# State space groups of a two-block layer: decay arguments by TensorE instead of reloaded rows, centre tap on ScalarE

## The reference, cut to what matters

```python
def depthwise_conv(u, w, b):                     # 5 taps, centre tap is k = 2
    y = lax.conv_general_dilated(u, w.astype(u.dtype), window_strides=(1,), padding=[(pad, pad)], ...)
    return y + b.astype(u.dtype)

def segsum_exp(a):
    cs = jnp.cumsum(a, axis=-1)
    diff = cs[..., :, None] - cs[..., None, :]
    ...
    return jnp.exp(jnp.where(mask, diff, -jnp.inf))      # mask: lower triangle

def ssd_scan(x, dt, a, b, c):
    ...
    xdt = x * dt[..., None]
    decay = segsum_exp(a_dt)
    cb = jnp.einsum('bclgn,bcsgn->bcgls', c, b)
    y_diag = jnp.einsum('bcgls,bcgrls,bcsgrp->bclgrp', cb, decay, xdt)
    decay_states = jnp.exp(a_cs[..., -1:] - a_cs)
    states = jnp.einsum('bclgn,bcgrl,bclgrp->bcgrpn', b, decay_states, xdt)
    ...                                                   # scan over the 4 chunks
    y_off = jnp.einsum('bclgn,bcgrpn,bcgrl->bclgrp', c, prev, jnp.exp(a_cs))
    return (y_diag + y_off).reshape(Bsz, S, G, R, P)
```

## Time and profile before

| | us |
|---|---|
| median of 3 runs (lowest, highest) | 2027.85 (2026.93, 2028.11) |
| the profiled execution itself | 2022.01 |
| its span in the trace | 2020.2 |
| PE busy | 1840.2 (91%) |
| DVE busy | 971.5 (48%) |
| ACT busy | 795.3 (39%) |
| POOL busy | 842.3 (42%) |
| mean granted clock of PE | 0.964 of full |

### The profile page before, as it was taken

The page is one execution under the profiler, slowest core; times in us unless marked ns, Lnnn a source line. Parts: engine busy times, 40 slices in busy tenths (PEclk is TensorE's granted clock), DMA queues, the critical chain, the costliest instruction groups (busy, mean ns, idle before and its releaser), DMA issues.

```text
span 2020.2 us, 27117 instructions
## 1 busy us (share of the span) xinstructions
PE 1840.2 (91%) x8948; PEld 1517.4 (75%) x8948; DVE 971.5 (48%) x1312; ACT 795.3 (39%) x1627; POOL 842.3 (42%) x598
## 2 busy tenths in 40 slices
PE   5598898899789999998899999999989999889988
PEld 4477777677578787877788888877878888777766
DVE  4389888999930555423532022232082211545654
ACT  4233333333232465532343233334433332456542
POOL 4244443344734312243454444444484444442212
PEclk9899999999889999999999999999999999999989
DMA  4742223323113311132233323323222223221101
GB/s 153 137 145 60 87 89 98 104 83 104 42 53 94 110 60 61 52 136 75 82 94 94 101 98 94 96 92 136 93 83 84 83 85 103 73 87 33 62 31 52
DMA packets 55011, 176.76 MB, mean 87 GB/s; under 512 B 5291, under 2 KB 7723, under 8 KB 54668
## 3 DMA queue, kind: packets, MB, share of 16 engines
q1 hardware_dynamic: 38592, 140.53, 21.8%
q10 hardware_dynamic: 16332, 35.11, 6.4%
HBM read 169.19 MB, written 6.42 MB: 87 GB/s over the span
## 4 chain that ended last, share of the span: by engine, by line
PE 61%; DVE 19%; issue 12%; POOL 3%; ACT 3%; ACTq 1%; DVEq 1%; DMA 0%; POOLq 0%
PE main L294 47%; DVE dmat L1747 4%; PE aux L754 3%; PE main L322 2%; POOL w_lo L257 2%; DVE u_acc L1716 2%; PE aux L619 1%; PE aux L741 1%; DVE y_all L1787 1%; PE aux L728 1%; PE aux L364 1%; DVE dmat L1752 1%; DVE x_res L536 1%; PE aux L729 1%; PE aux L1628 1%
## 5 line engine op out<-in xcount | busy, mean ns | idle before, releaser
L257 POOL TENSOR_TENSOR w_lo<-raw,w_hi 128x512 fp32r<-128x512 f32 x504 | 708.0, 1411 | 1044.3 <-ACT w_hi L253 1026.7
L253 ACT ACTIVATE w_hi<-raw 128x512 fp32r<-128x512 f32 x486 | 302.5, 630 | 713.0 <-PE main L294 708.2
L294 PE MATMUL main<-w_hi,a_hi 128*128 128x512 f32 x752 | 320.2, 426 | 2.3 <-ACT vv L1350 1.4
L294 PE MATMUL main<-w_hi,a_lo 128*128 128x512 f32 x752 | 300.9, 400 | 0.0
L294 PE MATMUL main<-w_lo,a_hi 128*128 128x512 f32 x752 | 300.7, 400 | 0.0
L294 PE MATMUL main<-a_hi,w_hi 128*128 128x512 f32 x640 | 259.7, 406 | 2.2 <-ACT u_raw L1159 2.2
L294 PE MATMUL main<-a_hi,w_lo 128*128 128x512 f32 x640 | 252.5, 394 | 0.0
L294 PE MATMUL main<-a_lo,w_hi 128*128 128x512 f32 x640 | 252.4, 394 | 0.0
L294 PEld LDWEIGHTS main<-w_hi,a_lo 128*128 128x128 f32 x752 | 145.7, 194 | 32.5
L294 PEld LDWEIGHTS main<-w_hi,a_hi 128*128 128x128 f32 x752 | 146.5, 195 | 30.4 <-issue 1.9
L294 PEld LDWEIGHTS main<-w_lo,a_hi 128*128 128x128 f32 x752 | 146.6, 195 | 24.5
(11 more groups left out here) (278 smaller groups left out, 2997.8 us busy)
## 6 DMA issues: line engine op xcount, KB each, us to landing
raw<-w_stream_in SPq DMA_DIRECT2D x264, 512.0 KB, 3.5
dmat<-cs_rows ACTq DMA_DIRECT2D x32, 512.0 KB, 9.1
x_res<-x_in ACTq DMA_DIRECT2D x8, 512.0 KB, 4.9
rel_rows<-rel_row ACTq DMA_DIRECT2D x1, 4096.0 KB, 44.8
bias<-rel_rows ACTq DMA_DIRECT2D x2, 1536.0 KB, 7.8
out<-x_res SPq DMA_DIRECT2D x4, 512.0 KB, 2.6
bgate<-b_gate_in ACTq DMA_DIRECT2D x4, 256.0 KB, 5.7
ln_g<-ln_g_in ACTq DMA_DIRECT2D x1, 1024.0 KB, 6.7
```

The lines of the kernel that those rows point to most:

```text
L253: eng.activation(w_hi[:, k, :], raw[:, k, :], ACT.Copy).then_inc(hi_done, 1)
L257: eng.tensor_tensor(w_lo[:, k, :], raw[:, k, :], w_hi[:, k, :].bitcast(F32), ALU.subtract).then_inc(lo_done, 1)
L294: mm = eng.matmul(mb[m][:, :], lhs, rhs, start=(first and k == 0 and n == 0), stop=(last and k == KT - 1 and n == 2))
```

## The change

The cumulated sums no longer go through HBM.
- The transposed sums (64 rows: direction, group, head) are kept on chip in `cs_hl`: a rounded high part in partitions 0 to 63 (ACT copy) and the remainder in 64 to 127 (DVE). `pick` is a 0/1 table whose column (direction, group, head) has ones at the row of that high part and of its remainder; `pick_rows` copies a group's 8 columns into `picked`.
- `pe_arg(g, r)` is new on PE: one picked column, broadcast to 128 columns as the stationary operand, times `cs_hl` spreads head r's row over all partitions, direction 0 into aux2 and direction 1 into aux3. It takes both banks, so it waits for both `aux_free`, and whoever uses the banks next waits for `arg_done`.
- `take_arg` on ACT copies aux2 into e_buf with the (negated) per-token sum as bias, one instruction for each of the 4 chunks. `arg_min` on DVE adds the other direction's per-token sum to aux3 and takes the minimum with e_buf, again one instruction per chunk. Then `decay_exp` and `weigh` go on as before; dmat only holds weigh's result.
- `load_decay` and its waits are gone. ACT's wait for the bias rows of the later attention (`rel_stored`) now stands behind the last group.
- `centre` puts the centre tap and the bias of the convolution on ACT (Identity with scale and bias); DVE's `conv` keeps the 16 other taps.
- Each engine's list is written anew: arguments 0 and 1 of a group are made during the group before (slots 8 and 10), 2 and 3 in the group itself (slots 1 and 4).

```diff
+        cs_hl = at("cs_hl", B0 + 60 * KB, [P, TOK], FR)
+        pick = at("pick", B0 + 63 * KB, [P, 64])
+        picked = at("picked", B0 + 63 * KB + 256, [P, 2, 2, R], FR)
...
-        def load_decay(eng, g, r):
-            ...
-            eng.dma_start(dmat[r][:, :, :], src).then_inc(decay_landed[r], 16)
...
+        def pe_arg(eng, g, r, half):
+
+            if r == 0:
+                eng.wait_ge(pick_set, g + 1)
+
+            if not (isinstance(g, int) and g == 0 and r == 0):
+                for b in range(2):
+                    eng.wait_ge(aux_free[b], g * 5 + r)
+            for dr in range(2):
+                one_row = picked[:, half, dr, r:r + 1].broadcast_to((P, P))
+                x = eng.matmul(ab[2 + dr][:, :], one_row, cs_hl[:, :], start=True, stop=True)
+            x.then_inc(arg_full, 1)
+
+        def pe_turn(eng, g, part, half):
             bank = part % 2
+            eng.wait_ge(arg_done, g * 4 + (part // 2 + 1))
...
+        def pe_states(eng, g, i, half):
             if i == 0:
                 eng.wait_ge(xw_done, g * 2 + 2)
+            eng.wait_ge(arg_done, g * 4 + (3 + i // 2))
...
+            def centre(g, taken, pair):
+
+                two = TILES[2 * pair:2 * pair + 2]
+                act.wait_ge(bank_free, taken + (max(two) + 1))
+                for m in two:
+                    act.activation(u_acc[:, m, :], u_raw[:, m, :], ACT.Identity, bias=par[:, bass.ds(g * 4 + (PC["conv_b"] + m), 1)],
+                                   scale=par[:, bass.ds(g * 20 + (PC["conv_w"] + m * 5 + 2), 1)]).then_inc(centred, 1)
+
+            def take_arg(g, r):
+
+                act.wait_ge(arg_full, g * 4 + (r + 1))
+                if not (isinstance(g, int) and g == 0 and r < 2):
+                    act.wait_ge(t_done, g * 4 + (r - 1))
+                for c in range(NT):
+                    cs = slice(c * P, c * P + P)
+                    x = act.activation(e_buf[r % 2][:, cs], ab[2][:, cs], ACT.Identity, bias=cs_sb[:, c, bass.ds(g * R + r, 1)])
+                x.then_inc(arg_in, 1)
...
             take_x(0)
+            centre(0, 0, 0)
+            centre(0, 0, 1)
             hi(2, range(0, 3))
+            take_arg(0, 0)
             for n in range(4):
                 silu(0, n)
             hi(2, range(3, 6))
-            act.wait_ge(cs_stored, 16)
-            for r in range(R):
-                load_decay(act, 0, r)
             take_turned(0, 0)
+            take_arg(0, 1)
             hi(2, range(6, 7))
             take_turned(0, 2)
             take_turned(0, 3)
             take_x(1)
             hi(2, [7])
+            decay_exp(0, 0)
+            decay_exp(0, 1)
...
                     silu(g + 1, 2)
                     silu(g + 1, 3)
+                    take_arg(g + 1, 0)
                     slots(9, 10)
                     take_turned(g + 1, 0)
                     slots(10, 11)
+                    take_arg(g + 1, 1)
                     if half == 1:
                         take_x(gp * 3 + (P_Z + 2))
+                    decay_exp(g + 1, 0)
+                    decay_exp(g + 1, 1)
                     slots(11, 12)
                     take_turned(g + 1, 2)
                     take_turned(g + 1, 3)
...
+            def arg_min(g, r):
+
+                dve.wait_ge(arg_in, g * 4 + (r + 1))
+                for c in range(NT):
+                    e = e_buf[r % 2][:, c * P:c * P + P]
+                    x = dve.scalar_tensor_tensor(e, ab[3][:, c * P:c * P + P], cs_sb[:, c, bass.ds(g * R + (NH + r), 1)], e,
+                                                 ALU.add, ALU.min)
+                x.then_inc(arg_done, 1)
...
-                decay(0)
-                decay(1)
                 weigh(0)
+                if not last:
+                    pick_rows(g + 1, 1 - half)
+                arg_min(g, 2)
                 weigh(1)
-                decay(2)
-                decay(3)
                 take_states(0)
                 take_states(1)
+                arg_min(g, 3)
                 weigh(2)
+                take_states(2)
                 weigh(3)
-                take_states(2)
```

106 lines of the change are left out of this document (54 added, 52 removed).

## The result

| | before | after |
|---|---|---|
| median of the timed runs, us | 2027.39 (2024.29 to 2028.11, 4 runs) | 2041.12 (2038.06 to 2043.38, 4 runs) |
| profiled execution / its span, us | 2022.01 / 2020.2 | 2043.38 / 2041.3 |
| last group's y is complete (first transpose of the next stage on PE) | 559.66 | 577.43 |
| from there to the end of the span | 1460.5 | 1463.9 |
| DVE / ACT busy, us | 971.5 / 795.3 | 883.0 / 859.2 |

The ratio is 1.007 (95% interval 1.0052 to 1.0087): slower by 0.7%, 14 us by the medians. The forecast was 2018, the range ended at 2032. DVE lost 88 us of work and the program became longer all the same. The stage that was changed took 17.8 us more; the 3.4 in the rest lie behind the edited code, and over the fourteen profiles of this study that rest lay between 1460.3 and 1464.7.

What follows compares the result with a forecast made beforehand. The order of waits between DVE and PE was taken as the bound; start -15.4, group 0 +0.9, odd groups -0.3, even +7.8, groups 5 and 6 +3.0, last -6.5 gave -10.5: 2018 us, range 2003 to 2032.

Steps and rivals of the forecast that it cites:

- -15.4: Start: without the loads of cumulated sums, group 0's states begin at 100.0 instead of 115.36 us.
- neither is idle enough to be written off, so the order of waits decides: Bound: in a 57.8 us group DVE is busy 52.4 and PE 52.0, so wait order counts, not busy share.
- +7.3: Closing, last convolution tap to next group's last turn (transposes of a convolved tile): 12.4 us instead of 5.1.
- 2.25: Each leg, ACT's four argument copies then DVE's four minima, takes 2.25 us, bounds 1.7 and 2.5.
- Rival D: Small instructions do not overlap: leg 2.5 us, 0.25 more on 19 legs; 2024 us, chance 0.12.
- B: Serial closing and even opening: legs cost 0.65 more, DVE's fetch gap stays, weigh late; about +21, 2039 us, chance 0.20.
- -4.1: Middle of odd groups, states to first tap: 17.4 us instead of 21.5.
- -1.7: Taps stretch, odd and even groups: 1.7 us shorter without the two centre taps on DVE.
- weigh 1.3 to 2.6: Opening of a group: DVE's weigh takes 1.3 to 2.6 us, as it meets POOL.
- -5.0: Middle of even groups: 18.9 us instead of 23.9, with 1.5 allowed for PE's low clock.
- Rival C: Start: ACT waits for weights while bias rows hold the queues; 2028 us, chance 0.10; sign: group 0's states after 105.
- A: Closings and openings: PE keeps its clock through the closing wait and weigh escapes POOL; -14, 2004 us, chance 0.20.

Runs made afterwards that it cites:

- early_xtok_pick: Kernel after with both leading arguments and cb's masking under the second pair's taps, x_tok copies before table load and exponentials, pick copy after second state update: 1992.84 us, ratio 0.9826.
- early_both: Kernel after with the next group's minima for heads 0 and 1 and the masking of cb under the second convolution pair's taps: 2017.93 us, ratio 0.9964.
- before_centre: Kernel before with only the convolution's centre taps and bias moved to ACT: 2017.66 us, ratio 0.9965.
- centre_back: Kernel after with the convolution's centre taps and bias put back on DVE: 2053.68 us, ratio 1.0145.
- pick_late: Kernel after with the pick copy moved from ahead of minimum 2 to behind the second state update: 2043.63 us, ratio 1.0095.

## Why the prediction was wrong

**The forecast in one line** was -10.5 for the stage; it became +17.8. The miss of 28 has four parts: start 5.1 (states at 105.06, not 100.0), group 0 behind its states 2.1 (+3.0 for +0.9), groups 1 to 6 18.3 (+28.8 for +10.5), last group 2.8 (-3.7 for -6.5).

**The step that failed.** The places of the waits were right; what failed is the pricing of the stretches between them. I added DVE's and POOL's durations mostly as they are undisturbed and gave the hand-offs between engines next to nothing. An odd group came out 4.2 longer than my sum (opening 1.1, middle 1.4, taps 1.3, closing 0.4), an even one 2.0 (opening 0.7, middle -0.1, taps 0.6, closing 0.8). The second failed term is the start, -15.4: it took the centre taps out of the chain to the first turns, where they stayed as a wait for ACT.

**Bounds, "neither is idle enough to be written off, so the order of waits decides": right**, and stronger than I used it. early_xtok_pick changes only the order and moves the stage end by 48 us.

**Closing, "+7.3": right in place and nearly in size.** 12.8 and 13.2 for 12.4. PE's wait was 6.4 to 6.7 for "some 6", and it did restart slowly. The row of the closing shows a clock of 0.73, so part of it at the lower level of 1.2 GHz, where the three other stretches of that group have 1.00:

```profile
331.50:344.30 12.80, 9.76 (x42) 8.23 (x43) 6.16 (x14) 6.31 (x17) 2.55 (x2) 0.73 0.15 41
```

early_both shows that the dependency was the cause.

**Legs, "2.25": right** (1.14 + 1.13 = 2.27). Rival D's 2.5 was too dear; B's legs over 2.9 didn't come, nor did its fetch gap of 1.8. B's time, 2039, was nearest by far, and the two places it named, serial closing and even opening, are the two whose repair pays; its mechanism for the price was wrong, so its number is luck.

**Middle and taps, "-4.1" and "-1.7" in odd groups: failed.** They became -2.7 and -0.4. In the middle of the odd group the states start at 292.94 and argument 3's matmuls at 303.73, 0.35 later than mine; DVE's minimum ends 3.3 behind that, where I had 0.46 + 2.25, so 0.6 for two hand-offs between engines; and the two state updates with their waits took 2.35 for my 1.4 (even group: the multiplication 1.48 at 372.28). That is 1.9, less 0.2 for quicker products: 1.7, 0.3 more than the 1.4 that the whole stretch was longer, so the parts are not exact. In the taps three pairs of off products and y adds take 7.7 (318.07 to 325.76), 6.6 before: the y adds at 319.19 need 1.84 for two, beside a w_lo of POOL. Products in the openings met xw: their mean over all is 1837 ns, 1324 in the earlier trace rows.

```profile
L1804 DVE TENSOR_TENSOR dmat<-cb_m,e_buf 128x1024 f32<-128x1024 f32 x29 | 53.3, 1837 | 2.7 <-ACT e_buf L1188 2.5
```

POOL in the kernel after:

```profile
319.22 1.54 POOL L258 TENSOR_TENSOR w_lo<-raw,w_hi 128x512 fp32r<-128x512 f32 x1 [3.61 <-ACT w_hi L254]
...
350.17 5.56 POOL L1057 TENSOR_TENSOR xw<-xdt,e_st 128x1024 f32<-128x1024 f32 x2 [1.26 <-DVE xdt L1845]
```

In the even groups the middle's -5.0 became -5.1, by luck: I had 1.5 in it for the low clock behind PE's wait, and the trace has the full clock there (1.00 from 356.8 to 375.6, behind a wait of 3.14), which made up for the same missing 1.4. The even taps, -1.7, became -1.1; in that group of the kernel before the second pair's centre taps took 1.00 and not 1.72, so there was less to remove.

before_centre shows such neighbours on the other kernel: of what DVE no longer had to do, more than half came back in longer neighbours. The Trainium skill has the pair of ports that DVE and GpSimd share as an exclusive lock, the loser waiting for the whole instruction ("SBUF — State Buffer", SBUF: two separate sides). The pick copy agrees: 1.87 beside xw and 0.30 away from it, and at 353.89 it ends (355.76) when xw does (355.73). "Minus the two centre taps" in full is the same error: centre_back puts all four taps at 1.9 a group, where their rows had 3.3.

**Openings: odd 1.1 too low, even 0.7.** "weigh 1.3 to 2.6" was 2.92, two xw took 5.56 (their mean from 100 to 545 us rose from 2402 to 2761 ns), and "pick copies (under 0.2 us each)" were wrong by a factor of nine, if nearly harmlessly (pick_late: the even openings are 0.2 shorter).

**Start, "-15.4": became -10.3.** I had the convolutions end at 78.5 for losing their centre taps; they ended at 81.1. ACT's first copies came at 63.62, 1.2 later than before, behind the new work on cs_hl and cs_sb that stands ahead of rel_row. Its centre taps took 0.73 each for my 0.55, and two of them had to be done before DVE could begin, at 67.34 instead of 64.48. DVE's 16 taps then took 13.78, about 1 more than before:

```profile
63.62 2.07 ACT L1165 ACTIVATE u_raw<-main 128x512 f32<-128x512 f32 x4 [2.42 <-DVE rel_row L1749]
65.72 2.93 ACT L1172 ACTIVATE u_acc<-u_raw,par 128x512 f32<-128x512 f32 x4
```

```profile
67.34 13.78 DVE L1766 SCALAR_TENSOR_TENSOR u_acc<-u_raw,par,u_acc 128x510 f32<-128x510 f32 x16 [4.52 <-issue]
```

So the centre taps are not "hidden" there: no cover exists in group 0, and centre_back, with the taps on DVE, ends its convolution at the same time. The other half of the 5.1 arose behind it. In this execution PE's granted clock was 0.56 from 82.2 to 85 and 0.89 from there to 89.4, and PE waited 1.20 for b_tok (89.36). pick_late, with the same code up to there, had 1.00 from 81.5 to 87 and asked for that argument at 87.05; it waited the same 1.2. About 1.6 of the 5.1 is thus this execution's clock, and 0.7 its slightly later convolution. Rival C's check ("after 105") came true by 0.06 in this one execution and fails in six others (102.74 to 103.12); its late weights were not seen as the wait in any. Of the other rivals, A (the clock kept in the closing, 2004) fell with the 0.73 above.

**What the change is worth by parts.** Start -10.3; centre taps in the groups -13.3 (centre_back); the whole is +17.8, so the new way of forming the arguments costs 17.8 + 10.3 + 13.3 = 41 us in the groups, 6 a group. The repairs of its order (early_xtok_pick) bring back 46 behind group 0's states, with every operation still there. That the order of the operations decides is thus shown. The slower DVE and POOL instructions are not what came back: in early_xtok_pick the product's mean is 1856 ns and xw's 2819 (1835 and 2761 in the kernel after, 100 to 560 us). How the rest divides between the waits and the lower clock behind them is not taken apart, and no run takes out what DVE and POOL cost each other.

## What to carry to other kernels

Work taken from an engine is worth what the chain of waits gives back, not its busy time: before counting it, walk each new dependency through every engine's queue and ask what stands ahead of it there that nobody waits for, as the table load and exponentials did here. New links that begin only when a stretch is over (arguments behind the last tap) should be threaded into it; and take both links or expect a third. For durations on an engine that shares its port, use the neighbours' contended rows as well. Before you put a difference of 2 us down to an edit, look where in the trace it arises: the start moved by 2.3 us between executions of the same code, and one group of pick_late was 3 us longer than the others like it. And try the one-line repairs first: on the kernel before, two of them gave 0.9%, without any of the new machinery.
